# A fused two-block transformer on one core: gate at the PSUM copy, sums into x, stores by token tile, transposes ahead of modulation products, identity products in TensorE's waits

## What is computed

```python
# first block
x = x + g1 * (merged @ w_o)
h = rms_norm(x, norm2_g) * (1 + sc2) + sh2
x = x + g2 * hierarchical_moe(h, ...)       # 32 experts, top 2 of 8 in the best of 4 groups
x = rms_norm(x, final_g)
# second block, layer 0 and 1; mod = silu(c) @ ada_w[layer] + ada_b[layer], split in six
u = x * (1 + sc1) + sh1
x = layernorm(alpha * x + (1 + g1) * mixer(u), ln1_g, ln1_b)
u = x * (1 + sc2) + sh2
ff = dense_swiglu(u) if layer == 0 else moe_swiglu(u)     # 8 experts, top 2
x = layernorm(alpha * x + (1 + g2) * ff, ln2_g, ln2_b)
```

## Time and profile before

| what | value |
|---|---|
| median of 3 runs | 2145.06 us (2142.33 to 2147.05) |
| the profiled execution | 2147.18 us |
| its span | 2145.5 us |
| TensorE busy | 1987.7 us (93%) |
| VectorE busy | 578.2 us (27%) |
| ScalarE busy | 197.4 us (9%) |
| mean granted clock of TensorE | 0.966 |
| HBM read | 653.76 MB |

### The profile page before, as it was taken

How to read it: one execution, slowest core, us unless ns; L and a number is a source line. 1 busy time by engine, 2 the same in 40 slices (tenths; PEclk the granted TensorE clock), 3 DMA queues, 4 the chain that set the end, 5 groups by cost and what they waited for, 6 DMA issues and landing times.

```text
span 2145.5 us, 68168 instructions
## 1 busy us (share of the span) xinstructions
PE 1987.7 (93%) x31213; PEld 1604.6 (75%) x31213; DVE 578.2 (27%) x1318; ACT 197.4 (9%) x320; POOL 19.0 (1%) x69
## 2 busy tenths in 40 slices
PE   6999979999999989989999899799899998999995
PEld 4777557778777757648677576589898998989993
DVE  4204242223222342353324424501011010110105
ACT  2112020000000001000000010111010100101010
POOL 1000000000000000000000000000000000000000
PEclk9999989999999999999999899799999999999997
DMA  9797659999999994327757433199999999999990
GB/s 352 235 360 285 223 206 375 421 424 421 421 420 423 424 387 167 118 101 277 260 213 261 167 118 118 56 373 377 394 380 379 387 381 394 370 391 386 365 395 20
DMA packets 245796, 655.78 MB, mean 306 GB/s; under 512 B 17348, under 2 KB 38244, under 8 KB 237540
## 3 DMA queue, kind: packets, MB, share of 16 engines
q1 hardware_dynamic: 237200, 647.41, 79.5%
q0 software_dynamic: 1456, 5.24, 0.7%
q10 hardware_dynamic: 7076, 2.20, 0.4%
HBM read 653.76 MB, written 1.05 MB: 305 GB/s over the span
## 4 chain that ended last, share of the span: by engine, by line
PE 81%; DMA 11%; DVE 4%; SPq 2%; issue 2%; ACT 0%; DVEq 0%
PE ps L1531 79%; DMA ring<-in_moe_w_up_dram 11%; SPq L425 2%; PE ps L1539 2%; DVE hT L885 1%; DMA ring<-in_w_ada_dram 1%; DVE x L964 0%; DVE stat L952 0%; DVE arena L1024 0%; DVE newton L865 0%; DVE newton L866 0%; DVE stat L867 0%; DVE x L935 0%; DVE x L1336 0%; DVE tok L1335 0%
## 5 line engine op out<-in xcount | busy, mean ns | idle before, releaser
L1531 PE MATMUL ps<-arena,ring 128*64 128x80 f32 (+2 forms) x25216 | 888.2, 233 | 50.2 <-DMA ring<-in_moe_w_up_dram 45.5
L1531 PEld LDWEIGHTS ps<-arena,ring 128*64 128x64 f32 (+1 forms) x25216 | 873.6, 140 | 72.9 <-DMA ring<-in_moe_w_up_dram 49.7
L1531 PE MATMUL ps<-hT,ring 128*128 128x256 f32 (+1 forms) x1680 | 358.1, 385 | 4.2 <-DVE stat L889 2.2
L1531 PEld LDWEIGHTS ps<-hT,ring 128*128 128x128 f32 (+1 forms) x1680 | 307.3, 188 | 53.9 <-issue 8.0
L1531 PE MATMUL ps<-ring,arena 128*64 128x512 f32 (+1 forms) x880 | 273.6, 595 | 1.5 <-DVE stat L1451 1.1
L1531 PE MATMUL ps<-arena 128*128 128x128 f32 (+7 forms) x1296 | 232.2, 344 | 19.3 <-DVE arena L1388 5.6
L1531 PEld LDWEIGHTS ps<-ring,arena 128*64 128x64 f32 (+1 forms) x880 | 104.6, 159 | 151.3 <-issue 147.6
L1531 PEld LDWEIGHTS ps<-arena 128*128 128x128 f32 (+4 forms) x1296 | 160.2, 192 | 70.8 <-issue 42.1
L1275 DVE TENSOR_TENSOR arena<-arena,ps 128x160 f32<-128x160 f32 x88 | 28.2, 321 | 539.8 <-PE ps L1531 539.8
L1531 PE MATMUL ps<-ring,hT 128*128 128x512 f32 (+2 forms) x256 | 87.6, 500 | 0.0
L1211 DVE TENSOR_TENSOR tok<-tok,ps 128x512 f32<-128x512 f32 x104 | 71.5, 687 | 34.9 <-PE ps L1531 34.5
(11 more groups left out here) (304 smaller groups left out, 712.6 us busy)
## 6 DMA issues: line engine op xcount, KB each, us to landing
ring<-in_moe_w_gate_dram SPq DMA_DIRECT2D x160, 512.0 KB, 10.0
ring<-in_moe_w_up_dram SPq DMA_DIRECT2D x160, 512.0 KB, 7.1
ring<-in_moe_w_down_dram SPq DMA_DIRECT2D x160, 512.0 KB, 10.2
ring<-in_w_gate_dram SPq DMA_DIRECT2D x32, 2048.0 KB, 14.7
ring<-in_w_up_dram SPq DMA_DIRECT2D x32, 2048.0 KB, 14.1
ring<-in_w_down_dram SPq DMA_DIRECT2D x32, 2048.0 KB, 12.4
ring<-in_w_in_dram SPq DMA_DIRECT2D x19, 2048.0 KB, 12.9
ring<-in_w_ada_dram SPq DMA_DIRECT2D x12, 2048.0 KB, 17.1
```

Source lines behind the costliest of these rows:

```text
L1531: ins = pe.matmul(*args, **kw)
```

## The change

The gate g2 is applied where VectorE copies expert results from PSUM, the combine products are added to x and not to tok, and `gated_ffn` is gone. In layer 1 the ln1 gains and the factor alpha are applied to x at the head of the MoE2 branch (`gained_x`), not between the mixer and the router; the last norm is written out so that four passes do it with its gains, and each token tile is stored when ready. Behind MoE1 TensorE's transposes of x stand ahead of modulation chunks 9 to 11. `keep_busy(n)` is n products of identity with itself, 128x512 wide, into a free bank that nobody reads; 31 of them are put in at six points of the program. The diff without the branch for experts that don't fit:

```diff
-            sp.wait_ge(H["x_ready"], 1)
-            sp.dma_start(out[0].rearrange("(t p) d -> p t d", p=P), x[:, :, :]).then_inc(stored, 16)
-            sp.wait_ge(stored, 16)
+            for t in range(TT):
+                sp.wait_ge(tile_ready, t + 1)
+                sp.dma_start(out[0][t * P:(t + 1) * P, :], x[:, t, :]).then_inc(stored, 16)
+            sp.wait_ge(stored, 16 * TT)
...
             first_experts()
-            ada_copies(1, 9, ADA_CHUNKS)
             for layer in range(2):
                 act.wait_ge(H["scale_ready"], 3 + 2 * layer)
                 transposed(shift_col)
+                if layer == 0:
+                    ada_copies(1, 9, ADA_CHUNKS)
...
-            def combined(q, banks, i, k):
+            def combined(q, banks, i, k, last=False):
                 for c in range(4):
                     t, half = c // 2, c % 2
                     b = side(q, banks, i, k + c)
-                    dst = tok[:, t, half * CH:(half + 1) * CH]
+                    dst = x[:, t, half * CH:(half + 1) * CH]
                     side_free(q, banks, dve.tensor_tensor(dst, dst, ps[:, b, :], ALU.add), i, k + c)
+                    if last:
+                        ins = stats(x, t, half)
+                if last:
+                    ins.then_inc(x_stats, 1)
...
-                        ins = dve.tensor_copy(y_slot[0:width, half * CH:(half + 1) * CH], ps[0:width, 4 + half, :])
+                        cols = slice(half * CH, (half + 1) * CH)
+                        ins = dve.tensor_tensor(y_slot[0:width, cols], ps[0:width, 4 + half, :], gB[0:width, 1, cols], ALU.mult)
...
+            def gained_x():
+                dve.wait_ge(got_rows, ROWS_LN2)
...
+                            ins = dve.tensor_tensor(x[:, t, :], x[:, t, :], one, op)
...
+                    ins = dve.tensor_scalar(x[:, t, :], x[:, t, :], ALPHA, None, ALU.mult)
...
+                dve.memset(stat[:, 124:125], 0.0).then_inc(H["rows_used"], 1)
...
                 dve.memset(stat[:, 127:128], 0.0).then_inc(q["y_free"], 1)
+                gained_x()
                 with dve.Fori(0, NE2) as i:
...
-                        ins = dve.tensor_copy(yT[:, 4 * half:4 * half + 4, :],
-                                              ps[:, 4 + half, 0:4 * cap].rearrange("p (a b) -> p a b", a=4))
+                        ks = slice(4 * half, 4 * half + 4)
+                        ins = dve.tensor_tensor(yT[:, ks, :], ps[:, 4 + half, 0:4 * cap].rearrange("p (a b) -> p a b", a=4),
+                                                gate_col[:, ks].unsqueeze(2).to_broadcast([P, 4, cap]), ALU.mult)
...
-                combined(q, SIDE2, NE2, 2)
+                combined(q, SIDE2, NE2, 2, True)
...
-            gated_ffn(1.0)
             ins = rms(x)
...
-            ada_columns(1, 8, ADA_CHUNKS)
-            dve.wait_ge(v_free, nv[0])
             for layer in range(2):
                 if layer == 0:
                     modulate(colC[:, 0, :], None, SC1, SH1, 1)
+                    ada_columns(1, 8, ADA_CHUNKS)
+                    dve.wait_ge(v_free, nv[0])
...
-                    gain_x()
...
+                    step(dve.tensor_scalar(gate_col[:, :], sec(G2, 2), 1.0, None, ALU.add))
...
-                    gated_ffn(ALPHA)
+                    dve.wait_ge(x_stats, 1)
...
+                    for t in range(TT):
+                        step(dve.scalar_tensor_tensor(out=x[:, t, :], in0=x[:, t, :], scalar=stat[:, 108 + 2 * t:109 + 2 * t],
+                                                      in1=rowB[:, 0, :], op0=ALU.subtract, op1=ALU.mult), wait=False)
+                    step(dve.tensor_copy(stat[:, 80:82], stat[:, 108:112].rearrange("p (a b) -> p a b", b=2)[:, :, 1]))
+                    rstd(stat[:, 82:84], stat[:, 80:82], 1.0, LN_EPS)
+                    for t in range(TT):
+                        dve.scalar_tensor_tensor(out=x[:, t, :], in0=x[:, t, :], scalar=stat[:, 82 + t:83 + t],
+                                                 in1=rowB[:, 1, :], op0=ALU.mult, op1=ALU.add).then_inc(tile_ready, 1)
...
+            def keep_busy(n):
+                pe.wait_ge(v_free, nv[0] - 3)
+                for _ in range(n):
+                    mm(ps[:, nv[0] % 4, :].rearrange("p (a b) -> p a b", a=4), ident[:, :],
+                       ident[:, :].unsqueeze(1).to_broadcast([P, 4, P]), start=True, stop=True)
...
+                if layer == 0:
+                    keep_busy(3)
                 pe.wait_ge(H["chosen_ready"], layer + 1)
...
                 last.then_inc(v_full, 1)
+                keep_busy(5)
...
             for layer in range(2):
+                if layer:
+                    keep_busy(6)
                 token_transposes(x, 1 + 4 * layer)
...
                 free(2)
+                keep_busy(6)
                 token_transposes(x, 3 + 4 * layer)
```

64 lines of the change are left out of this document (46 added, 18 removed).

## The result

| | before | after |
|---|---|---|
| median, us | 2146.06 (2142.33 to 2150.37, 4 runs) | 2132.23 (2129.93 to 2134.25, 4 runs) |
| profiled execution, us | 2147.18 | 2134.25 |
| its span, us | 2145.5 | 2132.4 |
| mean granted clock | 0.966 | 0.975 |

The ratio is 0.993, with a 95% interval of 0.9915 to 0.9944. The changed kernel is faster by 0.7%; the forecast was 2126, with a range of 2118 to 2137, and the time lies inside it, 6 us above the forecast (and at the slow end of the 2121 to 2133 that the sum alone gave). By the spans of the two profiled executions the difference is 13.1 us, where the sum had 19.5.

What follows compares the result with a forecast made beforehand. It took TensorE and full DMA engines to bound the kernel, with gains only at the joints between stages. Its terms summed to -19.5 us against a median of 2145.06, forecasting 2126 us, range 2118 to 2137.

Steps and rivals of the forecast that it cites:

- Router to MoE1: Before MoE1: three and five identity products fill TensorE's waits, so the first dispatch runs at full clock; -2.4 us.
- MoE1 to layer 0: Behind MoE1: four removed VectorE passes norm x 5.0 us earlier, but newly exposed work leaves half; -2.6 us.
- Mixer to FFN: Layer 0: six identity products, covered by a 6.03 us wait, speed the transposes and FFN's first records; -2.0 us.
- The first rival: At four joints: the clock falls again between identity products and real work; 2136 us, chance 12%.
- FFN to layer 1: Between FFN and layer 1: six identity products stand on the path, costing 7.6 us and giving back 3.2; +4.5 us.
- Router to MoE2: Layer 1's router to MoE2: earlier router chain, warm dispatch and warm first unit, together 9.0 us, taken as -8.0 us.
- (b): MoE2's dispatch, 7.12 us cold, runs at full clock like MoE1's 3.84; 3.3 us saved.
- (a): Layer 1's router: its products and transposes end earlier and VectorE's four gain passes are gone from there; 3.0 us saved.
- (c): MoE2's first unit, which had run at half clock until about 1392.5, runs warm; 2.7 us saved.
- the second rival: Both expert loops don't move forward since transfers set their ends, losing the gains before them; 2136 us, chance 10%.
- `gained_x` and its rows: Head of MoE2: six VectorE passes are covered, but 1 MB of ln2 rows now loads inside the loop; +0.5 us.
- The end: After the last combine sum: VectorE's remaining work takes 8.6 us, the split store leaves 3.2; -9.5 us.

Runs made afterwards that it cites:

- e7: Changed kernel with one 1 MB final store that waits for both token tiles, in place of two stores; 2131.96 us, ratio 0.9933.
- e3_no_products: Changed kernel with none of the 31 identity products; 2138.04 us, ratio 0.9953.
- e4: Changed kernel with the last layer norm's rows loaded into tok ahead of MoE2, not inside its loop; 2132.09 us, ratio 0.9923.
- after_again: The changed kernel itself, unaltered, measured once more; 2131.87 us, ratio 0.9924.
- e8: Changed kernel with layer 1's six identity products ahead of their wait and more identity products at waits where the clock fell; 2124.36 us, ratio 0.9893.
- e1: Changed kernel without the six identity products between the FFN and layer 1; 2129.22 us, ratio 0.9906.
- e2: Changed kernel with layer 1's six identity products moved ahead of the wait on the dense layer's last gate; 2127.6 us, ratio 0.9903.
- e9: The kernel of e8 with the last layer norm's rows also loaded ahead of MoE2; 2124.18 us, ratio 0.9885.
- e5: Kernel before the change with only the identity products added at their six places; 2151.57 us, ratio 1.0018.
- e6: Changed kernel with the modulation products ahead of the token transposes again behind MoE1; 2137.11 us, ratio 0.9948.
- e11: Changed kernel without identity products and with the old order behind MoE1, leaving VectorE's parts and the two stores; 2138.02 us, ratio 0.995.

## Why the prediction was right, and where its sum was off

The direction, the mechanism and the range held. The 6.4 us between -19.5 and -13.1 are these.

*Router to MoE1, -2.4, measured -1.0.* The dispatch lost its 2.84 us, and the waits behind the products are 0.68 and 0.46 us. What took 1.5 back is the router's row, 3.56 us at half clock where it was 2.06. It stands ahead of the first identity product: the clock came back at 284.5 where it had come back at 279.7, and in e7 it did so at 279.4 (A: 23.1, which is the -2.8 of the mechanism).

*MoE1 to layer 0, -2.6, measured -1.5.* VectorE's four passes were worth the 5 us that the sum gives them, and x stood ready 6.5 us behind the last sum. The transposes began 7.46 us behind the products and 0.05 behind VectorE's signal, so the 7.18 of the earlier trace rows and VectorE's chain end together, as the sum had it. The mis-sized term is what follows up to the end of the first chunk. I had 0.7 us for a chunk partly at half clock. The first chunk took 3.97 us, with the clock back only near 796.5. In e3_no_products, with the same instructions here, it took 1.92, and B is 21.2:

```profile
796.86 1.92 PE L1581 MATMUL ps<-ring,csT 128*32 128x512 f32 x16
```

In e4 and e7 the clock came back earlier than in the changed kernel, but a hole of 1.14 and 1.26 us without a semaphore stood inside the chunk, and B came out at 23.2 and 23.4 all the same. So this stage varies by 2 us for reasons that the sum didn't have. The Trainium skill's rule that was weighed at the earlier trace rows can be read here once more. In e7_one_store the transposes ran from 788.38 to 791.78, and the windows show 0.50 at 788 to 790 and then

```profile
790.00:792.00 2.00, 2.00 (x13) 1.68 (x13) 1.73 (x7) 1.55 (x5) 0.00 (x0) 0.66 1.06 387
792.00:794.00 2.00, 0.76 (x5) 0.00 (x0) 0.66 (x3) 1.34 (x4) 0.00 (x0) 1.00 0.55 203
```

0.66 over 2 us is a rise near 791.4, with transposes alone since 788.38. The Trainium skill, "TensorE: Matmul & The Clock Gate", "Part 4: PE-mode transpose", has it that work in transpose mode does not bring the full clock. By this trace it does, in e7 after 3 us; in the changed kernel the rise came 5.9 us behind their start, when products had joined.

*Mixer to FFN, -2.0, measured -2.35.* The transposes, 3.52 to 1.97, and the dense layer's head gave -2.35 together (from the mixer's end to the last `ones` product), the upper end. But inside the mixer 1.4 us were lost, and 1.5 in layer 1's: the small products behind a wait of 2.78 took 4.99 instead of 3.29 and 3.48 instead of 2.73. The wait is the same in both kernels; only the clock behind it differs: it fell 0.2 us before the end of that wait in the changed kernel (861.3), and 2.0 us behind it before (866.8). The rows are the same in after_again. The first rival, that the clock falls again, has come true in part: not at the FFN, once more at two of the joints that it named (below), and for the most part inside stages that the sum had left alone. These mixer rows and the router's row of MoE1 are worth 4.4 of the 6.4 us. For the mixers e8 shows that it was the clock: with products in that wait the row takes 2.73 in both layers. The change put no instruction at these places; why its traces have the slow rows and the one before has not, the runs don't say.

*FFN to layer 1, +4.5, measured +6.0.* The products took 7.74 for 7.6. That this term came out is partly luck. Its range rested on how long the clock had taken to come back elsewhere, and two of the three were misread: in the earlier trace rows it did come back, 6.0 us into the dispatch (0.95 in 300 to 302), and in the earlier trace rows it came back 13.3 us behind the start of the dispatch at 1379.23, with one wait of 0.81 us between, not 5.3 us behind the start of the work. Here it took 4.7 (0.96 in 1206 to 1207). Given back were 3.2 in the sum, but only 1.8 (transposes) and 0.4 (glow) in the trace, since the glow products were cold again, and the wait between them grew by 0.6; that case was in the bounds (+8). Stage D of e1 and e2, 16.8 and 16.0 beside 17.5 before, shows that all of it was avoidable.

*Router to MoE2, -8.0, measured -5.4 at the gate products and no more than that at MoE2's end.* (b) held: 7.12 to 3.80. (a) was 2.1, not 3.0: the clock held through the wait of 2.54 us and the router's row and fell at its end (0.96 in 1369 to 1370, 0.50 in 1370 to 1373), so that the transposes in front of ScalarE's copies took 3.63 us and the copies followed at 0.85 us apart. (c), 2.7 us for the first unit at full clock, failed outright. The unit was warm and the first up weights were asked for 4.75 us earlier (1394.19 for 1398.94), but the lead was 3.2 at the second (1409.40 for 1412.60) and 1.75 at the third (1426.81 for 1428.56), and 2.4 at the last combine products (2113.39 for 2115.79). A cold first unit had cost nothing, since TensorE waits 0.8 to 2.4 us for weights in each of the next units all the same. That is the second rival in small: what TensorE gains inside the stream's run the stream takes back, while what is gained ahead of it stays.

*`gained_x` and its rows, +0.5.* Nothing to be seen. VectorE's first product in MoE2 still had 0.55 us to wait for TensorE (it started at 1391.86), so the six passes were covered, and e4 and e9 find no difference beyond their intervals without the rows. F varies by more than that, 735.8 and 733.6 in two executions of one program. What MoE1 itself (-0.7) and F (-0.6) add to the 13.1 us is of that size.

*The end, -9.5, measured -10.3.* The passes came to 0.1 us (8.5 for 8.6), and the end behind them is 3.2, as taken. The rest lies in the other term: the kernel before had 4.5 us to the end of the span, counted from the write that raised `x_ready`, where I had the 4.0 of the store's landing, and I had begun 0.2 us behind the last sum.

*The third and fourth rivals.* The products did end up on the path in one place, not six, and cost 6.6 of the stage there. The whole is clear of no change.

## What to carry to other kernels

Filler work on a waiting engine must be issued ahead of the wait it fills, never behind it: the same six products cost 6.6 us of a stage on one side of a wait and nothing on the other. A small saving on one engine is worth only what the next engine's next hindrance leaves; here that was a hindrance that no semaphore explains (TensorE's first 5.9 to 7.2 us behind a branch; its cause is argued, not shown), and three parts of a change that bring -0.50, +0.18 and +0.08% alone bring -0.7% together, so neither a part's worth nor its harmlessness may be read from the whole. And before a cold unit is priced, look whether the unit behind it waits for a transfer: then warming it earns nothing.

## What the runs showed of the hardware

- Behind a branch, at the head of a new stage, TensorE stood 5.9 to 7.2 us after its last product before its work really began, in six kernels (before, e5, e6, e8, e9, e11). Within or behind the first chunk it stood once more for 0.7 to 2.1 us in six (before, e4, e5, e6, e7, e11), with no semaphore in the way, and not in the other eight. If it is kept busy until it leaves the branch, the stall is only moved: 5.10 us behind two transposes in e8, 5.09 in e9.
- The granted clock fell at the end of idle times of 2.2 to 2.8 us at some places (861.3 and 1212.9 in the changed kernel), fell 2 us behind them with TensorE at work at others (866.8 before, 1369.9 in the changed kernel), and held at others again: the 2.81 us ahead of the dense layer left it at 1.00 in the changed kernel, while in e1, with the same rows there, it was at 0.78 from 960 to 965.
- A 128x512 fp32 identity product on TensorE took 0.89 to 0.91 us at full clock (5.31 for six, 4.54 for five), a little more than the 0.87 of the earlier trace rows, and a chain of six that began cold 7.5 to 7.9.
- TensorE at work does not bring the clock back after a fixed time: it took 3.3 us from 955.72, 6.0 from 294.22 and 13.3 from 1379.23 in the kernel before (the last with one wait of 0.81 us inside), and 4.7 from 1201.37 in the changed kernel.
